# Router of a decoder layer on one core: rank products before the row transposes, routing tables by products with one-hot rows stationary

## The reference

```python
h = rms_norm(hres, norm2)
pg = softmax(h @ rg_w + rg_b)              # 4 groups
g_oh = one_hot(top_1(pg))
le = (h @ re_w + re_b).reshape(-1, 4, 4)   # 4 experts in each group
le_sel = einsum('ng,nge->ne', g_oh, le)
e_val, e_idx = top_k(le_sel, 2)
wts = softmax(e_val) * pg_top              # a weight for each of 2 experts
h_e = silu(h @ w1[e]) * (h @ w3[e])        # for each expert, width 256
y = hres + sum_e wts_e * (h_e @ w2[e])
```

## Time and profile before

| what | us |
|---|---|
| median of 3 runs | 840.67 |
| lowest, highest | 837.34, 842.12 |
| the profiled execution, its own time | 839.54 |
| its span (first to last instruction) | 837.7 |
| TensorE busy, share of the span | 795.4, 95% |
| VectorE busy | 384.5, 46% |
| mean granted TensorE clock | 0.979 |

### The profile page before, as it was taken

One profiled execution on the slowest core, in us unless ns is written; L12 is line 12 of the kernel. 1 busy time (PEld: TensorE's weight loads), 2 busy tenths in 40 slices (PEclk: granted clock), 3 DMA queues, 4 the chain that ended last, 5 costly groups with the idle time before them and its releaser, 6 DMA issues.

```text
span 837.7 us, 14312 instructions
## 1 busy us (share of the span) xinstructions
PE 795.4 (95%) x5314; PEld 566.5 (68%) x5314; DVE 384.5 (46%) x700; ACT 225.9 (27%) x427; POOL 278.6 (33%) x204
## 2 busy tenths in 40 slices
PE   9999999989999998999999999999999789999991
PEld 8887777666677786777776777788888544333330
DVE  4671676757478589555551311543311632020210
ACT  4122324331423634114313222422201512020110
POOL 0000421244654773335453545523000021342223
PEclk9999999999999999999999999999999979999996
DMA  9243632245555531345453541161156769999943
GB/s 369 91 145 93 211 101 77 76 143 159 170 182 178 166 120 63 91 143 166 145 164 114 166 163 64 63 215 65 51 202 251 297 228 377 391 378 386 371 148 48
DMA packets 72154, 147.23 MB, mean 176 GB/s; under 512 B 13207, under 2 KB 47016, under 8 KB 70036
## 3 DMA queue, kind: packets, MB, share of 16 engines
q1 hardware_dynamic: 65716, 135.43, 46.0%
q0 software_dynamic: 5920, 10.82, 5.2%
q10 hardware_dynamic: 448, 0.06, 0.1%
HBM read 137.71 MB, written 18.90 MB: 187 GB/s over the span
## 4 chain that ended last, share of the span: by engine, by line
PE 85%; DVE 8%; ACT 2%; DMA 2%; issue 1%; POOLq 0%; POOL 0%; SPq 0%; DVEq 0%; ACTq 0%
PE ps L854 21%; PE ps L578 13%; PE ps L1157 10%; PE ps L1061 7%; PE ps L823 7%; PE ps L1226 5%; PE ps L621 3%; PE ps L593 3%; PE ps L876 2%; PE ps L923 2%; PE ps L653 2%; PE ps L567 1%; PE ps L1146 1%; DMA tmp<-in_xT 1%; PE ps L709 1%
## 5 line engine op out<-in xcount | busy, mean ns | idle before, releaser
L578 PE MATMUL ps<-xn,ring 128*128 128x268 f32 (+1 forms) x576 | 138.4, 395 | 1.0 <-ACT qb L1319 0.9
L578 PEld LDWEIGHTS ps<-xn,ring 128*128 128x128 f32 x576 | 108.2, 192 | 26.1 <-issue 3.4
L2415 POOL TENSOR_TENSOR kv<-kv,sgd 128x1024 f32<-128x1024 f32 (+1 forms) x32 | 79.9, 2510 | 120.0 <-DVE tmp L1760 70.3
L1462 ACT ACTIVATE sgt<-sgt,vec 128x260 f32<-128x260 f32 x60 | 30.2, 511 | 143.5 <-DVE sgt L2022 79.3
L823 PE MATMUL ps<-br,ring 128*128 128x260 f32 x256 | 61.7, 388 | 2.1 <-DVE sgt L2026 1.3
L2505 POOL DMA_INDIRECT out_y<-cst,gtab x24 | 37.3, 1555 | 76.4 <-DVE cst L2340 35.7
L854 PE MATMUL ps<-xn,ring 128*128 128x260 f32 x240 | 58.8, 388 | 2.3 <-ACT cst L1319 1.3
L854 PE MATMUL ps<-xn,qb 128*128 128x260 f32 x240 | 57.7, 383 | 0.0
L1061 PE MATMUL ps<-qk,ring 128*128 128x260 f32 x256 | 56.5, 383 | 0.0
L823 PEld LDWEIGHTS ps<-br,ring 128*128 128x128 f32 x256 | 47.6, 190 | 12.9 <-issue 2.8
L1061 PEld LDWEIGHTS ps<-qk,ring 128*128 128x128 f32 x256 | 48.6, 190 | 7.8 <-issue 0.4
(11 more groups left out here) (474 smaller groups left out, 1468.4 us busy)
## 6 DMA issues: line engine op xcount, KB each, us to landing
ring<-in_w_mg SPq DMA_DIRECT2D x32, 640.0 KB, 4.3
kv<-in_kc SPq DMA_DIRECT2D x128, 128.0 KB, 2.1
kv<-in_vc SPq DMA_DIRECT2D x128, 128.0 KB, 2.1
ring<-in_w_in SPq DMA_DIRECT2D x24, 512.0 KB, 4.7
kv<-in_w SPq DMA_DIRECT2D x8, 1024.0 KB, 15.0
br<-in_w SPq DMA_DIRECT2D x7, 1024.0 KB, 14.8
sgd<-in_w SPq DMA_DIRECT2D x6, 1024.0 KB, 16.4
qk<-in_w SPq DMA_DIRECT2D x6, 1024.0 KB, 12.2
```

Of the source, the lines that this page charges most:

```text
L578: mm = pe.matmul(ps[:, 2 * (t % 2) + h, 0:hw], wsl(c, k), xnv[:, k, col0 + h * hw:col0 + (h + 1) * hw], start=(k == 0), stop=(k == KT - 1))
L1462: act.activation(g, g, ACT.Sigmoid, bias=vv(V_BM + 8 * "ABCD".index(n) + m + i)).then_inc(g_a, 1)
L2415: pool.tensor_tensor(kb, kb, qbc[:, b:b + 1, :].to_broadcast([P, HALF // 2 + (half and u), 256]), ALU.mult)\
```

## The change

- TensorE: `rows_of(hTr, 0, NB)` goes from ahead of the rank products to behind them. All five transposes of the residual now stand between the rank products and the first table.
- Table products: `oh_row` (128 columns) is stationary and `marks` (22 columns) is moving. The result is 128 partitions by 22 columns at once, so the copy to 64 partitions, the transpose and the copy back go away. The sum of the two choices is formed in PSUM (bank 4), and the second choice alone is formed again in bank 5: 15 products in place of 10. The weights need the sum alone: 10 products into bank 7, in place of bank 2.
- DVE: four of the ten `oh_row` come ahead of `marks`, and TensorE's first table product waits for all five. DVE reads the sum from PSUM for `from_row`; it then copies the second choice, clears its overflow columns and takes the difference for the first choice. The last two of these are new, and the sum on DVE and one copy go.
- The first `outputs` on TensorE waits for `g_ok`, since bank 7 is read for the weights before.

The diff, cut to its core:

```diff
-            rows_of(hTr, 0, NB)
 ...
-            for b in range(1, 3):
+            for b in range(NB):
                 rows_of(hTr, b, NB + b)
+
+            def by_rows(bk, j, b, mark, first, last):
+                return pe.matmul(ps[:, bk, 0:n_t], oh_row[0:RB, NB * j + b, :], marks[0:RB, mark, b, :], start=first, stop=last)
+
             for b in range(NB):
-                pe.wait_ge(oh_ok, 2 * b + 3)
+                pe.wait_ge(oh_ok, max(5, 2 * b + 3))
                 for j in range(2):
-                    mm = pe.matmul(ps[32 * j:32 * j + n_t, 5, 0:P], marks[0:RB, j, b, :], oh_row[0:RB, NB * j + b, :],
-                                   start=(b == 0), stop=(b == NB - 1), tile_position=(0, 32 * j))
+                    by_rows(4, j, b, j, b + j == 0, b + j == NB)
+                mm = by_rows(5, 1, b, 1, b == 0, b == NB - 1)
             mm.then_inc(tab_t[0], 1)
-            pe.wait_ge(sel_ok, 2)
-            pe.transpose(ps[:, 5, P:P + 64], slots[0:64], ident[0:64, 0:64]).then_inc(tab_tt[0], 1)
-            rows_of(hTr, 3, NB + 3)
-            rows_of(hTr, 4, NB + 4)
             pe.wait_ge(oh_ok, 2 * NB + 2)
-            pe.wait_ge(tt_a, NB + 3)
+            pe.wait_ge(tt_a, 2 * NB)
             for b in range(NB):
                 for j in range(2):
-                    mm = pe.matmul(ps[32 * j:32 * j + n_t, 2, 0:P], marks[0:RB, 2 + j, b, :], oh_row[0:RB, NB * j + b, :],
-                                   start=(b == 0), stop=(b == NB - 1), tile_position=(0, 32 * j))
+                    mm = by_rows(7, j, b, 2 + j, b + j == 0, b + j == NB)
             mm.then_inc(wts_t[0], 1)
 ...
+                if i == 0:
+                    pe.wait_ge(g_ok, 1)
 ...
-            dve.wait_ge(oh2_ok, 1)
-            tt(marks[R, 0:2], oh_tile[R], tokid[R]...).then_inc(oh_ok, 1)
             for b in range(NB):
+                if b == 2:
+                    dve.wait_ge(oh2_ok, 1)
+                    tt(marks[R, 0:2], oh_tile[R], tokid[R]...).then_inc(oh_ok, 1)
 ...
-            two_kinds(tab_t, 5)
-            dve.wait_ge(*tab_tt)
-            link(dve.tensor_copy(slots[:, 64:128], ps[:, 5, P:P + 64]))
-            link(tt(both, kinds[0], kinds[1], ALU.add))
+            dve.wait_ge(*tab_t)
+            both, second = ps[:, 4, 0:n_t], ps[:, 5, 0:n_t]
             link(ts(far, both, 0.0, float(FAR), ALU.is_equal, ALU.mult))
             stt(from_row[:, 0:n_t], both, -1.0, far, ALU.add, ALU.add).then_inc(tab_ok, 1)
+            link(dve.tensor_copy(late, second))
+            link(dve.memset(late[:, TILES:], 0.0))
+            link(tt(early, both, late, ALU.subtract))
 ...
-            two_kinds(wts_t, 2)
-            dve.wait_ge(*wts_tt)
-            link(dve.tensor_copy(slots[:, 64:128], ps[:, 2, P:P + 64]))
-            tt(g_w[:, 0:n_t], kinds[0], kinds[1], ALU.add).then_inc(g_ok, 1)
+            dve.wait_ge(*wts_t)
+            dve.tensor_copy(g_w[:, 0:n_t], ps[:, 7, 0:n_t]).then_inc(g_ok, 1)
```

More of the change, by code:

```diff
@@ L314, in program @@
         tt_t, tt_a, route_t = sem("tt_t"), sem("tt_a"), sem("route_t")
-        lgm, rank_ok, tab_t, tab_tt, wts_t, wts_tt = [(route_t, i + 1) for i in range(6)]
+        lgm, rank_ok, tab_t, wts_t = [(route_t, i + 1) for i in range(4)]
         rw_ok, lg_t, lg_a, lg_d = sem("rw_ok"), sem("lg_t"), sem("lg_a"), sem("lg_d")
@@ L1115, in _ @@
             pe.matmul(ps[:, 5, 0:NB * NE], every, selm, start=True, stop=True).then_inc(rank_ok[0], 1)
-            for b in range(1, 3):
+            for b in range(NB):
                 rows_of(hTr, b, NB + b)
+            def by_rows(bk, j, b, mark, first, last):
+                return pe.matmul(ps[:, bk, 0:n_t], oh_row[0:RB, NB * j + b, :], marks[0:RB, mark, b, :], start=first, stop=last)
             for b in range(NB):
-                pe.wait_ge(oh_ok, 2 * b + 3)
+                pe.wait_ge(oh_ok, max(5, 2 * b + 3))
                 for j in range(2):
-                    mm = pe.matmul(ps[32 * j:32 * j + n_t, 5, 0:P], marks[0:RB, j, b, :], oh_row[0:RB, NB * j + b, :],
-                                   start=(b == 0), stop=(b == NB - 1), tile_position=(0, 32 * j))
+                    by_rows(4, j, b, j, b + j == 0, b + j == NB)
+                mm = by_rows(5, 1, b, 1, b == 0, b == NB - 1)
             mm.then_inc(tab_t[0], 1)
-            pe.wait_ge(sel_ok, 2)
-            pe.transpose(ps[:, 5, P:P + 64], slots[0:64], ident[0:64, 0:64]).then_inc(tab_tt[0], 1)
-            rows_of(hTr, 3, NB + 3)
-            rows_of(hTr, 4, NB + 4)
             pe.wait_ge(oh_ok, 2 * NB + 2)
-            pe.wait_ge(tt_a, NB + 3)
+            pe.wait_ge(tt_a, 2 * NB)
             for b in range(NB):
                 for j in range(2):
-                    mm = pe.matmul(ps[32 * j:32 * j + n_t, 2, 0:P], marks[0:RB, 2 + j, b, :], oh_row[0:RB, NB * j + b, :],
-                                   start=(b == 0), stop=(b == NB - 1), tile_position=(0, 32 * j))
+                    mm = by_rows(7, j, b, 2 + j, b + j == 0, b + j == NB)
             mm.then_inc(wts_t[0], 1)
-            pe.wait_ge(sel_ok, 3)
-            pe.transpose(ps[:, 2, P:P + 64], slots[0:64], ident[0:64, 0:64]).then_inc(wts_tt[0], 1)
             def rows_T(u):
@@ L2277, in _ @@
             dve.wait_ge(idx2_ok, 1)
-            link(dve.tensor_reduce(tile_f[R, :], steps[R, :, 1:], X, ALU.add))
-            link(stt(row_f[R, :], tile_f[R, :], -float(P), pos_f[R, :], ALU.mult, ALU.add))
-            dve.wait_ge(oh2_ok, 1)
-            tt(marks[R, 0:2], oh_tile[R], tokid[R].unsqueeze(1).unsqueeze(3).to_broadcast([RB, 2, NB, n_t]), ALU.mult).then_inc(oh_ok, 1)
+            link(dve.tensor_reduce(row_f[R, :], steps[R, :, 1:], X, ALU.add))
+            link(stt(row_f[R, :], row_f[R, :], -float(P), pos_f[R, :], ALU.mult, ALU.add))
             for b in range(NB):
+                if b == 2:
+                    dve.wait_ge(oh2_ok, 1)
+                    tt(marks[R, 0:2], oh_tile[R], tokid[R].unsqueeze(1).unsqueeze(3).to_broadcast([RB, 2, NB, n_t]), ALU.mult)\
+                        .then_inc(oh_ok, 1)
                 for n in range(2):
                     ts(oh_row[R, NB * n + b, :], io_row[R], row_f[R, NB * n + b:NB * n + b + 1], None, ALU.is_equal).then_inc(oh_ok, 1)
-            def two_kinds(kind, bk):
-                dve.wait_ge(*kind)
-                dve.tensor_copy(slots[0:64, :], ps[0:64, bk, 0:P]).then_inc(sel_ok, 1)
-            two_kinds(tab_t, 5)
-            dve.wait_ge(*tab_tt)
-            kinds = [slots[:, 64 + 32 * j:64 + 32 * j + n_t] for j in range(2)]
-            link(dve.tensor_copy(slots[:, 64:128], ps[:, 5, P:P + 64]))
-            both, far = io_row[:, 0:n_t], io_row[:, 32:32 + n_t]
-            link(tt(both, kinds[0], kinds[1], ALU.add))
+            far, far2, late, early = [io_row[:, 32 * k:32 * k + n_t] for k in range(4)]
+            dve.wait_ge(*tab_t)
+            both, second = ps[:, 4, 0:n_t], ps[:, 5, 0:n_t]
             link(ts(far, both, 0.0, float(FAR), ALU.is_equal, ALU.mult))
             stt(from_row[:, 0:n_t], both, -1.0, far, ALU.add, ALU.add).then_inc(tab_ok, 1)
+            link(dve.tensor_copy(late, second))
+            link(dve.memset(late[:, TILES:], 0.0))
+            link(tt(early, both, late, ALU.subtract))
             link(dve.reciprocal(one[15], one[15]))
@@ L2301, in _ @@
             tt(marks[R, 2:4], oh_tile[R], rt[R, 15:17, :, 0:1].to_broadcast([RB, 2, NB, n_t]), ALU.mult).then_inc(oh_ok, 1)
[L2302 to L2305, removed]
+            for rows, out in ((early, to_row), (late, to_row2)):
+                link(ts(far2, rows, 0.0, float(FAR), ALU.is_equal, ALU.mult))
+                link(stt(out[:, 0:n_t], rows, -1.0, far2, ALU.add, ALU.add))
             link(tt(ecmp, eend.unsqueeze(1).to_broadcast([P, OVER, NE]),
```

## The result

| | median us | executions | lowest, highest |
|---|---|---|---|
| before | 840.75 | 15 | 837.34, 844.00 |
| after | 843.31 | 15 | 840.90, 845.61 |

The ratio of after to before is 1.0029, with a 95% interval of 1.0017 to 1.0041: 2.4 us slower (the medians are 2.6 apart), where 0.9 us faster was forecast. The time is outside the stated range, by 0.5 us.

What follows compares the result with a forecast made beforehand. The path was taken as mostly TensorE, with the router's chain to the source table and gather setting later work. Terms -0.96 + 0 + 1.28 - 1.22 gave -0.90 us, then 0 behind it: 839.8 us, range 836.2 to 842.8.

Steps and rivals of the forecast that it cites:

- Term 1: Rank products ahead of the residual's transposes: they start earlier, -0.96 us, bounds 0 and -1.1.
- Term 2: The residual's five transposes together behind the rank products: hidden by VectorE's chain, 0 us, with 1.4 us in hand.
- Term 4: From the table products to the source table: 1.62 us becomes 0.40, -1.22, bounds -1.1 and -1.25.
- VectorE ahead of the products: One-hots and marks ahead of the first table: TensorE's first table product moves from 668.51 to 669.01 us.
- The gather met an empty queue: Gather behind the source table: its data move some 1.5 us after issue, so it meets an empty queue as before.
- term 3: First table's thirty passes at 0.095 us each: VectorE called +1.28 us later; bounds +0.85 and +1.7, far end +4.4.
- Term 5: Behind the source table: the weights' table is hidden or late by some tenths, 0 us, bound +0.5.
- rival (b): Clock down through the first table and at the experts: +1.2 us, 840.7, at most +4.7; chance 0.18.

Runs made afterwards that it cites:

- e1: The kernel before with only the residual's block 0 transposed behind the rank products, tables as before: ratio 0.9998 to the kernel before (0.9977 to 1.0019).
- e10: The changed kernel with the sum's products signalled before the second choice's, and unused products in TensorE's idle stretches; 22 columns moving: ratio 1.0015 to the kernel before.
- e7: The changed kernel with 110 columns moving, the sum's products signalled first, and unused products in TensorE's idle stretches: ratio 1.0005 to the kernel before.
- e3: The changed kernel with products whose results nobody uses put in TensorE's idle stretches around the tables and ahead of the experts: ratio 1.0024 to the kernel before.
- e11: The changed kernel with 110 columns moving and the sum's products signalled first, without unused products: ratio 1.0016 to the kernel before.
- e8: The kernel before with rank products ahead of the residual's block 0 and unused products in idle stretches, old tables: ratio 0.9974 to the kernel before.
- e12: The same kernel as e8 run again, rank products first, old tables, unused products: ratio 0.9971 to the kernel before (0.9952 to 0.9991).
- e4: The kernel before with unused products in TensorE's idle stretches, 8 ahead of the first table: ratio 0.9991 to the kernel before (0.9970 to 1.0011).
- e2: The changed kernel with the residual's block 0 back ahead of the rank products, so new tables only: ratio 1.0053 to the kernel before.

## Why the prediction was wrong, point by point

**Right.** Term 1, the rank products: -0.96 forecast, -1.05 measured, and -1.09 at the source table with that edit alone (e1). Term 2, the residual's transposes together: they end at 667.3 with the first table at 669.2, hidden, though with 1.9 us in hand and not 1.4. Term 4, the copies gone: -1.22 forecast, 1.62 to 0.40 measured. One comparison behind it was misread: the read of the ranks has 80 columns against 22 in the new reads, so it is larger and not four fifths as large; the term stands all the same. VectorE ahead of the products: +0.50 forecast, +0.35 measured. The gather met an empty queue as before, 4.6 us from issue to landing against 4.7.

**The step that failed is term 3**, the thirty passes: +1.28 on record, +2.85 in the trace (from VectorE's read of the ranks to its call by the first table, 10.96 in place of 8.11). It was mis-sized twice.

- The pace at full clock. I took 0.095 a pass "between" two rows; the pair with the very same stationary shape had 0.11, and 0.11 it was, for moving sides of 22 (0.112 in e10) and 110 columns (0.115 in e7). At these short moving sides the pace went by the stationary side: 0.09 for 104 columns, 0.11 for 128. The rule of the Trainium skill that was quoted against the change ("TensorE: Matmul & The Clock Gate", section "LDWEIGHTS (loading the stationary operand)"), 107 ns for 128 columns, is 5 to 7% under the 0.112 and 0.115, read as a spacing. The page gives it as the length of one load, and that was about 192 ns at full clock here (e7). This part of the miss is 29 x 0.017 = 0.5 us. It was inside the term's bounds (0.11 a pass, +1.7).
- The clock. Twelve of the thirty passes ran at 0.5, another 12 x 0.11 = 1.3 us. This took the term beyond +1.7, towards its far end of +4.4.

With all passes at full clock the sum for this execution would be -1.05 + 0.35 + (4.78 - 1.3 - 2.28 = 1.20) - 1.22 = -0.72 at the source table, near the -0.90 on record. With the clock it is +0.59.

**Term 5 failed too**: 0 on record, +2.10 in the trace. "Hidden, or late by some tenths" was right for the wait itself: the second table ended 0.5 past the gather. What was left out is that the stretch behind it, transposes of the gathered rows and first experts, runs at the clock that the tables leave. From the source table to the first expert product it took 8.64 in place of 7.65 (+0.99), and from there to the second quad 25.75 in place of 24.64 (+1.11).

The parts add up: +0.59 + 0.99 + 1.11 = +2.69 in the two traces, where the ratio gives 2.4. Of this I put 1.3 + 0.99 + 1.11 = 3.4 down to the clock, and all else is -0.7. That fits the time at half clock: 17.0 us for 10.2 in the two traces, where the 6.8 more are worth 3.4 at most, and 41.4 for 35 as a mean over the executions. So it was rival (b), the slower side, at 0.18, priced at +1.2 for its usual case and +4.7 at most. What spoke against it in the forecast was the shorter idle stretch ahead of the table (1.4 us for 4.2; 1.9 in the trace). That didn't decide it: in after the clock fell 2.1 us into the table, with TensorE busy all that time on passes that move 22 columns, and in e3, with only 0.6 us of idle time ahead of the table, it fell there too.

The range doesn't follow from its own recipe. Carried to the median as the forecast was, (b) at its lesser price plus 1.5 is 840.67 + 1.2 + 1.5 = 843.4, and the low end is 840.67 - 2.4 - 1 = 837.3; counted from the profiled execution they are 842.2 and 836.1. The 842.8 on record is neither, and 843.4 would have held the 843.31 that was measured. The high end also took no account of (b) at its far price.

**Still open.** What exactly lowers the clock is shown only in parts: e7 against e10 and e11 show that with the new tables it took both wide passes and filled idle stretches to keep it up, but each has one profile, and where the clock falls differs between executions. Why e3's time stayed at 1.0024 with its quad under that of before isn't explained. Nor is it why e7's median is 1.7 us above e8's, timed beside it: both spend 30 us at half clock, e7's quad is the earlier by 1 us, and both traces wait for the last weights. So that the weights' stream is all that holds e7's time back isn't shown. And e1's gain in the trace isn't seen in its median, within an interval that is wider than the gain.

## What to carry to other kernels

Price a small product by its stationary side. Twenty passes with 128 columns stationary took 2.48 us at full clock (e7), twenty with 22 columns stationary, side by side in two column groups, 1.28 (e12). And passes of the first kind, though they followed each other without a gap, left the clock at half for the long products behind them. A short serial phase on TensorE ahead of a long dense one is worth reading by its granted clock, and unused products in its gaps can be worth as much as shortening it: the quad came 2 us earlier in e4's trace. In the time the gain is told from nothing only together with the earlier rank products (e8, e12). Before a gain is carried to the end, look at the last transfer that the dense phase needs, and at what releases it: its slack was 2.6 us in before's trace.

## What the runs showed of the hardware that I had not expected

- The pace of table passes is nearly the same for 22 and 110 moving columns, 0.112 (e10) and 0.115 us (e7) at 2.4 GHz, with 104x128 stationary; at 1.2 GHz it is 0.21 (e2).
- The granted clock fell to 0.50 in the middle of the first table, 2.1 us after TensorE had begun on it without a gap (1.9 us idle before), and stayed there through the second table, where TensorE was busy 4.40 of 4.40 us.
- Sixteen expert passes took 1.92 at full clock and 3.64 at half, so 17.0 us at half clock against 10.2 were enough to turn a gain of 0.7, by the sum above, into a loss of 2.7.
- A wait of 1.46 us near the end was followed by a clock of 0.50 for 3.4 us and cost 1.7 us more in the passes behind it (e7). A wait of 1.59 us at the same place cost nothing more: the clock stayed at 1.00 (e8).
